# A 16-head sparse attention stage joined to the input product in front of it, and a block boundary placed after a down projection

## The chip, the cores and the metric

The kernel runs on one core of a Trainium2 chip. A core has five instruction streams that run side by side and meet only at semaphores: TensorE (PE, matrix products and transposes), VectorE (DVE), ScalarE (ACT), GpSimd (POOL) and SyncE (SP, which issues the DMAs). The metric is the device time of one execution in microseconds, lower is better.

## What is computed

Two transformer blocks over 512 tokens of width 1024. The change touches the second block: its first mixer `mixer_ab`, and the place behind its first feed-forward part. Cut to what matters:

```python
def mixer_ab(h, w_in, ...):
    xr, gr, q, kc, vc, ks, vs, kw, vw, gl = jnp.split(h @ w_in, splits, axis=-1)
    y_rnn = rg_lru(causal_dwconv(xr, conv_w, conv_b), w_r, b_r, w_i, b_i, lam) * jax.nn.gelu(gr)
    y_att = nsa(q, kc, vc, ks, vs, kw, vw, gl, ...)     # 16 query heads, 4 key heads
    return jnp.concatenate([y_rnn, y_att], axis=-1) @ w_out

def rg_lru(x, ...):                                     # the recurrence
    ...
    u = jnp.sqrt(-jnp.expm1(2.0 * log_a)) * (i * x)
    ...                                                 # h_t = a_t * h_(t-1) + u_t, a scan over the 512 tokens

# nsa, for each token: gated sum of three attentions
    o = g[..., 0:1] * o_c + g[..., 1:2] * o_s + g[..., 2:3] * o_w   # compressed, 4 chosen blocks, window of 256

for i in range(2):                                      # second_block
    x = x + (1.0 + g_m) * rms_norm(mixer(h), norm_mix_post[i])
    h = rms_norm(x, norm_ffn_pre[i]) * (1.0 + sc_f) + sh_f
    x = x + (1.0 + g_f) * rms_norm(conv_ffn(h), norm_ffn_post[i])
```

## The kernel before

Activations are feature-major: a tile is 128 features by 512 tokens. A product walks over its output tiles; each takes 8 or more weight tiles, each split into a high and a low part (L327, L329, on DVE, from the six-slot `ring` into the three-slot `high`), and three matmuls per weight tile (L375 to L377, `passes`).

The program is a row of *blocks*. A block holds a program for each engine, and at its end all engines wait for one another (a barrier). `together` makes one block out of several stages: every engine runs its part of stage 1, then of stage 2, and so on, and only semaphores order the engines. The order on an engine is the order in which the code is written; nothing reorders it. Between blocks `k.next_stages()` starts a new set of semaphores, and `clear_previous` has POOL set the old ones to zero.

Three blocks matter here. **Block A** holds `ffn_up(0)`, `down_0`, the normalization `double_edge`, and `ab_front`: the input product `ab_in` (37 output tiles) with the recurrence and the compressed attention woven between its tiles. In `ab_front`, `evacuate(j)` (ACT, L2580) copies output tile j out of PSUM. The recurrence has 8 tiles of channels. Its last steps for each tile i are: `root` (ACT, square root, L2641), `open_out` (ACT, GELU of the gate, L2645), `scan` (DVE, one multiplication L2827 and the scan L2828), `multiply` (POOL, L2907), `high_part` (ACT, rounding to the high half, L2649) and `low_part` (DVE, the low half by subtraction, L2832). For tiles 4 to 7 the scans, and for all tiles `high_part` and `low_part`, stand behind the last output tile of the product, each in a loop of its own.

**Block B** is `sparse_attention`. It has 64 *items*: 8 pairs of heads (p), 4 groups of 128 query tokens (i), and b = 0 (chosen blocks) or 1 (window). Item m = 8p + 2i + b. Its width is the number of 128-key pieces: i + 1 for b = 0, at most 3 for b = 1, so that the widths of a pair are 1, 1, 2, 2, 3, 3, 4, 3. What an item needs:

- `scores` (PE, L2969): two matmuls into PSUM;
- the two reductions (DVE, L3053): add the mask, find the row maximum, write `rows`;
- two exponentials (ACT, L3084) with row sums;
- `norm` (DVE): a reciprocal (L3029) and two scalings (L3034);
- `transposes` (PE, L2982), `keep` (ACT, L3072, a copy out of PSUM), `values` (PE, L3004; the first of a pair also L2997).

The step m of each engine's program is, in this order:

```
PE:  scores(m+2)   transposes(m)   values(m-1)
DVE: reductions(m) norm(m-1)
ACT: exponentials(m)  keep(m-1)
```

Once a pair, ACT also runs `move` (L3077) and DVE `divide` (L387, L388). POOL writes the masks of the chosen blocks (`sel_bias`, L2950 and L2956) for pairs 0 to 3 at the start and for pairs 4 to 7 later. The masks lie in `k.high`, the place of the weights' high parts, which is free then.

**Block C** holds everything behind: `ab_out`, `ffn_norm_1` (an `edge`), `up_1`, `down_1`, `sc_norm` (an `edge`), the short convolution, two more products, `up_2`, `down_2` and the output. An `edge` (L463) is the passage from one product to the next. PE sums squares (L485, L488), ACT takes the root (L508), DVE inverts it (L530), PE spreads it (L477), and so on; `keep_busy` (L668) fills PE's gaps. ACT writes the last squares and the last output tile of the product ahead (L2333, L2335 in `plain_product`).

## Time and profile before

| | us |
|---|---|
| median of 3 runs | 2582.23 (2580.28 to 2588.74) |
| the profiled execution: time, span | 2582.75, 2580.9 |
| block B with the barrier ahead of it, on PE | 1360.6 to 1514.0 |
| PE busy in the whole span | 2417.4 (94%) |
| DVE, ACT, POOL busy | 1754.6 (68%), 665.7 (26%), 196.4 (8%) |

The profile is one execution; times in it are counted from the start of its span. A row of a timeline gives start, duration, engine, line and operation; in brackets stands how long the engine was idle before and whose instruction ended that. A barrier shows as a wait for a branch (L191 is the end of a block made by `together`). Instructions are pipelined: one may start shortly before the record of the one ahead ends.

### The profile page before, as it was taken

What the parts mean: (1) busy time and instruction counts of PE and PEld (TensorE: products, weight loads), DVE (VectorE), ACT (ScalarE), POOL (GpSimd) and SP (SyncE); (2) the same over time, 40 slices, a digit from 0 to 9 for tenths busy, and PEclk for the clock granted to TensorE, in tenths of its full rate; (3) what the DMA queues carried; (4) which work ended last, traced back from release to release, by engine and by line L of the source; (5) the groups of instructions that cost most, each with busy time, mean ns of one, the idle gap of its engine ahead of it and who ended that gap; (6) DMA issues with size and microseconds to landing.
All of it is one profiled execution on the core that took longest, in us unless ns stands there. A gap on an engine that the chain in (4) does not pass through costs nothing. (4 is left out here: it accounts for less than half of the span.)

```text
span 2580.9 us, 34064 instructions
## 1 busy us (share of the span) xinstructions
PE 2417.4 (94%) x13808; PEld 1957.6 (76%) x13808; DVE 1754.6 (68%) x2720; ACT 665.7 (26%) x1234; POOL 196.4 (8%) x169
## 2 busy tenths in 40 slices
PE   8997767798999999999988989999999999999997
PEld 6885766596688888787765568888888888888886
DVE  7674663774788886557787867766666886666653
ACT  3212432102111120221466741322211212322200
POOL 0002430200100001000021001000010001000000
PEclk9998976899999999999998999999999999999999
DMA  5220001241223345422220036233375353233342
GB/s 187 74 66 1 3 2 50 82 139 58 66 90 98 98 136 192 137 91 74 62 69 1 2 109 225 66 98 98 93 245 176 113 192 128 74 98 98 119 139 68
DMA packets 70332, 252.80 MB, mean 98 GB/s; under 512 B 7808, under 2 KB 8096, under 8 KB 69664
## 3 DMA queue, kind: packets, MB, share of 16 engines
q1 hardware_dynamic: 69888, 250.08, 29.4%
q8 instruction: 110, 1.80, 0.3%
q10 hardware_dynamic: 288, 0.54, 0.1%
q14 instruction: 46, 0.38, 0.0%
HBM read 248.50 MB, written 2.10 MB: 97 GB/s over the span
## 5 line engine op out<-in xcount | busy, mean ns | idle before, releaser
L375 PE MATMUL psum<-rounded_n,rounded_high 128*128 128x512 f32 x1856 | 738.5, 398 | 5.1 <-DVE rounded_n_low L559 1.8
L376 PE MATMUL psum<-rounded_n_low,rounded_high 128*128 128x512 f32 x1856 | 725.8, 391 | 0.0
L377 PE MATMUL psum<-rounded_n,rounded_ring 128*128 128x512 f32 x1856 | 725.5, 391 | 0.0
L329 DVE TENSOR_TENSOR rounded_ring<-ring,rounded_high 128x1024 fp32r<-128x1024 f32 (+1 forms) x360 | 444.6, 1235 | 12.4
L375 PEld LDWEIGHTS psum<-rounded_n,rounded_high 128*128 128x128 f32 x1856 | 350.8, 189 | 86.5 <-issue 8.5
L376 PEld LDWEIGHTS psum<-rounded_n_low,rounded_high 128*128 128x128 f32 x1856 | 350.8, 189 | 77.5 <-issue 5.8
L377 PEld LDWEIGHTS psum<-rounded_n,rounded_ring 128*128 128x128 f32 x1856 | 350.5, 189 | 73.8
L327 DVE CAST rounded_high<-ring 128x1024 fp32r<-128x1024 f32 (+1 forms) x360 | 246.4, 684 | 220.2 <-PE psum L377 211.7
L375 PE MATMUL psum<-rounded_arena,rounded_high 128*128 128x512 f32 x720 | 281.3, 391 | 4.4 <-DVE rounded_ring L329 4.4
L376 PE MATMUL psum<-rounded_arena,rounded_high 128*128 128x512 f32 x720 | 281.0, 390 | 0.0
L377 PE MATMUL psum<-rounded_arena,rounded_ring 128*128 128x512 f32 x720 | 280.9, 390 | 0.0
L2259 DVE SCALAR_TENSOR_TENSOR scratch<-arena,vecs,scratch 128x512 f32<-128x512 f32 x88 | 65.8, 748 | 162.8 <-ACT scratch L2246 162.8
L375 PEld LDWEIGHTS psum<-rounded_arena,rounded_high 128*128 128x128 f32 x720 | 135.7, 189 | 33.3 <-DVE rounded_ring L329 4.7
L376 PEld LDWEIGHTS psum<-rounded_arena,rounded_high 128*128 128x128 f32 x720 | 135.7, 188 | 28.2
L377 PEld LDWEIGHTS psum<-rounded_arena,rounded_ring 128*128 128x128 f32 x720 | 135.7, 188 | 28.2
L2240 ACT COPY arena<-psum 128x512 f32<-128x512 f32 x88 | 51.6, 587 | 351.2 <-PE psum L377 351.2
L2246 ACT ACTIVATE scratch<-arena,vecs 128x512 f32<-128x512 f32 x88 | 63.8, 725 | 201.1 <-DVE arena L2280 199.6
L2333 ACT ACTIVATE scratch<-psum 128x512 f32<-128x512 f32 x32 | 19.2, 600 | 322.0 <-PE psum L377 322.0
L428 POOL COPY sum_sq<-scratch 128x512 f32<-128x512 f32 x6 | 4.8, 802 | 1059.8 <-ACT scratch L2333 831.5
L431 POOL TENSOR_TENSOR sum_sq<-sum_sq,scratch 128x512 f32<-128x512 f32 x38 | 58.2, 1531 | 300.8 <-ACT scratch L2333 242.7
L785 DVE CUSTOM_DVE_ANT_0 arena<-arena 128x1024 f32<-128x1024 f32 x48 | 62.0, 1333 | 14.4 <-DMA arena<-in_mod_w 14.4
L785 DVE CUSTOM_DVE_ANT_0 n_low<-n_low 128x1024 f32<-128x1024 f32 x48 | 56.7, 1221 | 19.7 <-DMA n_low<-in_mod_w 19.7
(472 smaller groups left out, 3035.0 us busy)
## 6 DMA issues: line engine op xcount, KB each, us to landing
ring<-in_w_up SPq DMA_DIRECT2D x132, 512.0 KB, 3.5
ring<-in_w_down SPq DMA_DIRECT2D x48, 512.0 KB, 3.5
n_low<-in_mod_w SPq DMA_DIRECT2D x48, 512.0 KB, 5.5
arena<-in_mod_w SPq DMA_DIRECT2D x48, 512.0 KB, 5.3
ring<-in_w_ab_in SPq DMA_DIRECT2D x37, 512.0 KB, 3.5
ring<-in_w_mix_in SPq DMA_DIRECT2D x31, 512.0 KB, 3.5
ring<-in_w_sc_in SPq DMA_DIRECT2D x24, 512.0 KB, 4.9
ring<-in_w_down SPq DMA_DIRECT2D x24, 384.0 KB, 3.2
```

The lines of the kernel that those rows point to most:

```text
L327: nc.vector.tensor_copy(self.rounded(high), raw).then_inc(self.weights_rounded, 1)
L329: nc.vector.tensor_tensor(self.rounded(raw), raw, self.rounded(high), ALU.subtract).then_inc(self.weights_split, 1)
L375: self.nc.tensor.matmul(out, w_high, x_high, start=first, stop=False)
L376: self.nc.tensor.matmul(out, w_high, x_low, start=False, stop=False)
L377: return self.nc.tensor.matmul(out, w_low, x_high, start=False, stop=last)
L428: nc.gpsimd.tensor_copy(total, sq).then_inc(added, 1)
L431: nc.gpsimd.tensor_tensor(total, total, sq, ALU.add).then_inc(added, 1)
L785: k.nc.vector.tensor_tensor_reduce(out=self.tiles[:, i % 3], in0=self.tiles[:, i % 3], in1=self.cond, scale=1.0, scalar=0.0, op0=ALU.mult, ...
L2240: nc.scalar.copy(x, k.psum[:, j % PRODUCT_BANKS, :]).then_inc(out, 1)
L2246: nc.scalar.activation(dst, x, ACT.Copy, scale=taps[:, col:col + 1]).then_inc(tapped, 1)
L2259: link(nc.vector.scalar_tensor_tensor(dst, src[:, 0:T], taps[:, col:col + 1], dst, ALU.mult, ALU.add))
L2333: nc.scalar.activation(k.squares[:, j % 2, :], k.psum[:, j % PRODUCT_BANKS, :], ACT.Square).then_inc(squared, 1)
```

## The change

Four things.

1. `sparse_attention` becomes a stage of block A. The barrier between them goes. PE starts the first scores when all 37 output tiles are evacuated (`out`), the queries and keys are rotated and the values are kept; POOL's masks wait until the gates are made and the last product tile is used. `k.rows` lies in `k.n_low` in place of `k.scratch`, which the recurrence still holds.
2. The recurrence's last steps move into the first 12 steps of the attention. In steps 0 to 3 DVE runs the scans of tiles 4 to 7 behind `norm(m-1)`. In steps 4 to 11 ACT runs `high_part(m-4)` behind `keep(m-1)`, and DVE runs `low_part(m-4)`, which waits for it, behind `norm(m-1)`. POOL runs `multiply` of tiles 4 to 7 after the masks of pairs 0 to 3. The GELUs of tiles 4 to 6 go ahead of `evacuate(36)`, that of tile 7 behind it.
3. Block C is cut in two behind `down_1`; `sc_norm` and what follows form a block of their own. `sc_in`'s modulation no longer waits for that of `down_1`.
4. The DVE stages of a block share one semaphore for their step-by-step waits (`vector_link`) in place of one each. The scans get a semaphore `scaled` of their own.

```diff
@@ ab_front
             if j == 36:
                 for i in range(4, 8):
                     root(i)
+                for i in range(4, 7):
+                    open_out(i)
             evacuate(j)
-        for i in range(4):
-            high_part(i)
-        for i in range(4, 8):
-            open_out(i)
-        for i in range(4, 8):
-            high_part(i)
+        open_out(7)
+
+    def finish_scalar(act, step):
+
+        if step >= 4:
+            i = step - 4
+            act.wait_ge(multiplied, i + 1)
+            nc.scalar.copy(k.rounded(k.z[:, XR + i, :]), lru_t[i]).then_inc(halved, 1)
+
+    def finish_vector(dve, step):
+
+        if step < 4:
+            i = step + 4
+            dve.wait_ge(rooted, i + 1)
+            dve.wait_ge(gated_in, i + 1)
+            dve.wait_ge(risen_a, i + 1)
+            x = k.z[:, XR + i, :]
+            nc.vector.tensor_tensor(x, x, lru_t[i], ALU.mult).then_inc(scaled, 1)
+            dve.wait_ge(scaled, i + 1)
+            nc.vector.tensor_tensor_scan(lru_t[i], lru_r[i], x, 0.0, ALU.mult, ALU.add).then_inc(scanned, 1)
+        else:
+            i = step - 4
+            dve.wait_ge(halved, i + 1)
+            nc.vector.tensor_tensor(k.rounded(k.z[:, GR + i, :]), lru_t[i], k.rounded(k.z[:, XR + i, :]),
+                                    ALU.subtract).then_inc(lowered, 1)
...
-        for i in range(4, 8):
-            scan(i)
-        for i in range(KT):
-            low_part(i)
...
-        for i in range(KT):
+        for i in range(4):
             multiply(i)
...
+    def finish_pool(pool):
+        for i in range(4, KT):
+            pool.wait_ge(scanned, i + 1)
+            pool.wait_ge(gelu_done, i + 1)
+            nc.gpsimd.tensor_tensor(lru_t[i], lru_t[i], k.z[:, GR + i, :], ALU.mult).then_inc(multiplied, 1)
@@ sparse_attention, pool
+        pool.wait_ge(signals["gated"], TT)
+        pool.wait_ge(k.weights_used, k.product_done("ab_in", PRODUCTS["ab_in"][0] - 1))
...
+            if a == 0:
+                signals["finish_pool"](pool)
@@ sparse_attention, tensor
+        pe.wait_ge(signals["rotated"], signals["turned_parts"])
+        pe.wait_ge(signals["out"], signals["n_out"])
+        pe.wait_ge(signals["v_kept"], 4)
+        pe.wait_ge(signals["kept"], 4)
         scores(0)
         scores(1)
@@ sparse_attention, vector
             if m >= 1:
                 norm(m - 1)
+            if m < 12:
+                signals["finish_vector"](dve, m)
@@ sparse_attention, scalar
             if m >= 1:
                 keep(m - 1)
+            if m < 12:
+                signals["finish_scalar"](act, m)
@@ build
-        k.rows = k.scratch
-        k.next_stages()
-        sparse_attention(k)
+        k.rows = k.n_low
+        together(k, Stage(pool=k.clear_previous), up, down, norm, front, sparse_attention(k, front))
         k.next_stages()
...
         down_1 = plain_product(k, "down_1", k.hidden, k.n, mod, up_1)
+        together(k, Stage(pool=k.clear_previous), mixed, norm_1, up_1, down_1)
+        k.next_stages()
         norm_2 = edge(k, "sc_norm", down_1, mod_part(k, 0, 5), mod_part(k, 1, 1), mod_part(k, 1, 0), "sc_in", k.n)
...
-        together(k, Stage(pool=k.clear_previous), mixed, norm_1, up_1, down_1, norm_2, short, short_out, norm_3, up_2, down_2, norm_4,
+        together(k, norm_2, short, short_out, norm_3, up_2, down_2, norm_4,
                  store_output(k, norm_4))
```

In the orders below the lines are those of the changed kernel where the kernel after is shown: L2723 and L2725 are the multiplication and the scan (the scan is printed as SCALAR_TENSOR_TENSOR), L2713 is `high_part`, L2729 `low_part`, L3083 a reduction ("ISA"), L3059 and L3064 the reciprocal and scalings of `norm`, L3103 `keep`, L3115 an exponential, L2589 `evacuate`, L2654 `open_out`.

DVE before, from the last multiplication and scan of the recurrence to the first reductions of the attention:

```order
L2827 TENSOR_TENSOR arena<-arena,rstd 128x512
L2828 SCALAR_TENSOR_TENSOR rstd<-scratch,arena 128x512
L2832 TENSOR_TENSOR rounded_arena<-arena,rounded_arena 128x512 x4
L2832 TENSOR_TENSOR rounded_arena<-scratch,rounded_arena 128x512 x2
L2832 TENSOR_TENSOR rounded_arena<-sum_sq,rounded_arena 128x512
L2832 TENSOR_TENSOR rounded_arena<-rstd,rounded_arena 128x512
L191 UNCONDITIONAL_BRANCH
L3020 UNCONDITIONAL_BRANCH
L3053 ISA scratch,rest<-psum,high 128x128
```

DVE after, the end of step 3 and the whole of step 4:

```order
L3059 RECIPROCAL rest<-rest 128x2
L3064 TENSOR_SCALAR n_low<-n_low,rest,arena 128x256 x2
L2723 TENSOR_TENSOR arena<-arena,rstd 128x512
L2725 SCALAR_TENSOR_TENSOR rstd<-scratch,arena 128x512
L3083 ISA n_low,rest<-psum,high 128x384
L3083 ISA rest 128x1
L3083 ISA n_low,rest<-psum,high 128x384
L3083 ISA rest 128x1
L3059 RECIPROCAL rest<-rest 128x2
L3064 TENSOR_SCALAR n_low<-n_low,rest,arena 128x256 x2
L2729 TENSOR_TENSOR rounded_arena<-arena,rounded_arena 128x512
```

Each scan now stands between the scalings of one item and the reductions of the next, and the first subtraction stands behind the scalings of item 3.

ACT before, from the evacuation of the last output tile to the end of block A:

```order
L2580 COPY arena<-psum 128x512
L2649 CAST rounded_arena<-arena 128x512 x4
L2645 ACT_TABLE_LOAD
L2645 ACTIVATE arena<-arena 128x512 x4
L2649 CAST rounded_arena<-scratch 128x512 x2
L2649 CAST rounded_arena<-sum_sq 128x512
L2649 CAST rounded_arena<-rstd 128x512
L191 UNCONDITIONAL_BRANCH
```

ACT after, from the last GELUs over the start of the attention to step 5:

```order
L2654 ACTIVATE arena<-arena 128x512 x3
L2589 COPY arena<-psum 128x512
L2654 ACTIVATE arena<-arena 128x512
L3115 ACT_TABLE_LOAD
...
L3115 ACTIVATE n_low,rest<-n_low,rest 128x384 x2
L3103 COPY n<-psum 128x2x256
L2713 CAST rounded_arena<-arena 128x512
L3115 ACTIVATE n_low,rest<-n_low,rest 128x384 x2
L3103 COPY n<-psum 128x2x384
L2713 CAST rounded_arena<-arena 128x512
```

Three GELUs stand ahead of the last evacuation now, and each rounding stands behind the copy of the item's transposes.

## Rows read from the trace of the kernel before

**Rows 1.** The page's part 1: busy time of PE over the span

```profile
PE 2417.4 (94%) x13808; PEld 1957.6 (76%) x13808; DVE 1754.6 (68%) x2720; ACT 665.7 (26%) x1234; POOL 196.4 (8%) x169
```

**Rows 2.** Timeline of PE at the boundary of blocks A and B

```profile
1360.63 1.23 PE L2969 MATMUL psum<-arena 64*128 64x128 f32 x8 [16.46 <-PEq L191]
```

**Rows 3.** Timeline of DVE at the same boundary

```profile
1359.40 0.69 DVE L2832 TENSOR_TENSOR rounded_arena<-rstd,rounded_arena 128x512 fp32r<-128x512 f32 x1
1361.57 0.29 DVE L3053 CUSTOM_DVE_ANT_0 scratch<-psum,high 128x128 f32<-128x128 f32 x1 [1.48 <-PE psum L2969]
```

**Rows 4.** Timeline of ACT at the same boundary

```profile
1336.08 2.19 ACT L2645 ACTIVATE arena<-arena 128x512 f32<-128x512 f32 x4
...
1342.53 0.71 ACT L2641 ACTIVATE rstd<-rstd,floor 128x512 f32<-128x512 f32 x1
1344.21 0.58 ACT L2580 COPY arena<-psum 128x512 f32<-128x512 f32 x1 [0.98 <-PE psum L377]
...
1346.88 1.28 ACT L2645 ACT_TABLE_LOAD   x1
...
1350.47 0.62 ACT L2649 CAST rounded_arena<-scratch 128x512 fp32r<-128x512 f32 x1
```

**Rows 5.** Busy time by stretch: stretch, length, busy us of each engine, granted clock (PEclk)

```profile
1350.00:1356.00 6.00, 0.00 (x0) 0.00 (x0) 5.93 (x4) 2.27 (x5) 5.91 (x4) 0.50 0.00 0
...
1369.00:1373.00 4.00, 4.00 (x16) 1.99 (x16) 1.85 (x7) 1.29 (x4) 0.00 (x0) 0.50 0.00 0
1373.00:1377.00 4.00, 4.00 (x34) 2.18 (x30) 3.09 (x10) 2.58 (x8) 0.00 (x0) 0.97 0.02 4
...
1400.00:1410.00 10.00, 10.00 (x86) 5.55 (x84) 7.04 (x32) 7.40 (x25) 0.00 (x0) 1.00 0.01 2
```

**Rows 6.** Timeline of DVE in pair 1, block B: items 8 to 13

```profile
1380.21 0.28 DVE L3053 CUSTOM_DVE_ANT_0 scratch<-psum,high 128x128 f32<-128x128 f32 x1
...
1385.78 0.60 DVE L3034 TENSOR_SCALAR scratch<-scratch,rest,arena 128x128 f32<-128x128 f32 x2
...
1389.28 0.56 DVE L3053 CUSTOM_DVE_ANT_0 scratch<-psum,high 128x384 f32<-128x384 f32 x1 [0.96 <-PE psum L2969]
...
1390.24 0.16 DVE L3029 RECIPROCAL rest<-rest 128x2 f32<-128x2 f32 x1
...
1392.36 0.87 DVE L3034 TENSOR_SCALAR scratch<-scratch,rest,arena 128x384 f32<-128x384 f32 x2
```

**Rows 7.** Timeline of PE in pair 1: transposes of widths 1 and 4

```profile
1384.77 0.44 PE L2982 MATMUL psum<-consts,scratch 128*128 128x128 f32 x2
...
1398.38 1.09 PE L2982 MATMUL psum<-consts,scratch 128*128 128x128 f32 x8
```

**Rows 8.** Timeline of ACT in pair 1: `keep` of widths 1 and 3

```profile
1385.24 0.37 ACT L3072 COPY n<-psum 128x256 f32<-128x256 f32 x1 [0.45 <-PE psum L2982]
...
1394.16 0.80 ACT L3072 COPY n<-psum 128x768 f32<-128x768 f32 x1 [0.35 <-PE psum L2982]
```

**Rows 9.** Timeline of DVE at the first scans, without and with POOL beside it

```profile
1304.68 0.68 DVE L2827 TENSOR_TENSOR arena<-arena 128x512 f32<-128x512 f32 x1
1305.40 1.22 DVE L2828 TENSOR_TENSOR_SCAN arena<-arena 128x512 f32<-128x512 f32 x1
1306.54 1.72 DVE L2827 TENSOR_TENSOR arena<-arena 128x512 f32<-128x512 f32 x1
1308.29 2.20 DVE L2828 TENSOR_TENSOR_SCAN arena<-arena 128x512 f32<-128x512 f32 x1
```

**Rows 10.** Timeline of POOL beside those scans

```profile
1305.94 1.76 POOL L2902 TENSOR_TENSOR arena<-arena,scratch 128x512 f32<-128x512 f32 x1 [5.29 <-ACT scratch L2624]
```

**Rows 11.** Busy time by stretch, as in rows 5, of an early stretch of small matmuls

```profile
392.00:400.00 8.00, 7.16 (x49) 5.26 (x50) 1.42 (x5) 0.99 (x1) 0.00 (x0) 0.50 0.00 0
```

**Rows 12.** Timeline of PE behind `down_1`

```profile
1988.30 1.05 PE L485 MATMUL psum<-consts,sum_sq 128*128 128x128 f32 x8
```

**Rows 13.** Timeline of ACT behind `down_1`

```profile
1988.99 0.58 ACT L2335 COPY n<-psum 128x512 f32<-128x512 f32 x1
```

More of the change, by code:

```diff
@@ L2001, in residual_product @@
     nc = k.nc
-    out, squared, added, steps, done = (k.sem(f"{name}_{s}") for s in ("out", "squared", "added", "steps",
+    out, squared, added, done = (k.sem(f"{name}_{s}") for s in ("out", "squared", "added",
                                                                        "done"))
@@ L2202, in ffn_up @@
     both = idx == 0
[L2203 to L2204 removed]
+    out, padded, tapped, gate_done, risen, hid_done = (
+        k.sem(f"{name}_{s}") for s in ("out", "padded", "tapped", "gate", "risen", "hid"))
     taps = k.vec(f"ffn_conv_{idx}")
@@ new lines, in pool @@
+    def pool(pool):
+        pool.wait_ge(signals["gated"], TT)
+        pool.wait_ge(k.weights_used, k.product_done("ab_in", PRODUCTS["ab_in"][0] - 1))
+        made = 0
+        for a in range(2):
+            for i in range(TT):
+                if a:
+                    pool.wait_ge(maxed, 2 * (items.index((3, i, 0)) + 1))
+                for s in range(2):
+                    w = (i + 1) * P
+                    dst = k.sel_bias[s][i]
+                    nc.gpsimd.tensor_copy(
+                        dst[:, 0:w].rearrange("p (j x) -> p j x", x=HD),
+                        k.block_bias[:, i, 2 * a + s, 0:2 * (i + 1)].unsqueeze(2)
+                        .broadcast_to([P, 2 * (i + 1), HD])).then_inc(biased, 1)
+                    made += 2
+                    pool.wait_ge(biased, made - 1)
+                    nc.gpsimd.tensor_tensor(dst[:, w - P:w], dst[:, w - P:w], k.const("causal"), ALU.add
+                                            ).then_inc(biased, 1)
+            if a == 0:
+                signals["finish_pool"](pool)
@@ new lines, in vector, with norm, divide @@
+    def vector(dve):
+        link = Link(dve, steps)
+        def norm(m):
+            p, i, b = items[m]
+            w = keys(i, b)[1] * P
+            dve.wait_ge(risen, 2 * m + 2)
+            sums = k.stats[:, 1, row(m, 0):row(m, 0) + 2]
+            link(nc.vector.reciprocal(sums, sums))
+            for s in range(2):
+                h = 4 * group(p, s) + p % 4
+                e = k.rows[:, row(m, s), 0:w]
+                gate = k.gate_tok[:, i, 3 * h + 1 + b:3 * h + 2 + b]
+                nc.vector.tensor_scalar(e, e, k.stats[:, 1, row(m, s):row(m, s) + 1], gate,
+                                        ALU.mult, ALU.mult).then_inc(normed, 1)
+        def divide(p):
+            dve.wait_ge(moved, p + 1)
+            link(split(k, link, k.z[:, NQT + p, :], k.ab_low[:, p, :]))
+        for m, (p, i, b) in enumerate(items):
+            w = keys(i, b)[1] * P
+            dve.wait_ge(scored, m + 1)
+            if m >= ROWS:
+                dve.wait_ge(turned, m - ROWS + 1)
+            for s in range(2):
+                if b == 0:
+                    dve.wait_ge(biased, 2 * (2 * (p // 4 * TT + i) + s + 1))
+                    bias = k.sel_bias[s][i]
+                else:
+                    bias = k.const("window")[:, 384 - w:384]
+                nc.vector.tensor_tensor_reduce(
+                    out=k.rows[:, row(m, s), 0:w], in0=k.psum[:, 2 * (m % 2) + s, 0:w], in1=bias,
+                    scale=-scale, scalar=3e38, op0=ALU.add, op1=ALU.min,
+                    accum_out=k.stats[:, 0, row(m, s):row(m, s) + 1]).then_inc(maxed, 1)
+            if m >= 1:
+                norm(m - 1)
+            if m < 12:
+                signals["finish_vector"](dve, m)
+            if m % 8 == 5 and p >= 1:
+                divide(p - 1)
+        norm(len(items) - 1)
+        divide(PAIRS - 1)
@@ new lines, in scalar, with keep, move @@
+    def scalar(act):
+        def keep(m):
+            p, i, b = items[m]
+            w = keys(i, b)[1] * P
+            act.wait_ge(turned, m + 1)
+            if m >= PTS:
+                act.wait_ge(mixed, m - PTS + 1)
+            nc.scalar.copy(k.pt[:, 2 * (m % PTS):2 * (m % PTS) + 2, 0:w], k.psum[:, 4:6, 0:w]
+                           ).then_inc(kept, 1)
+        def move(p):
+            act.wait_ge(mixed, 8 * (p + 1))
+            nc.scalar.copy(k.ab_low[:, p, :], k.psum[:, 6 + p % 2, :]).then_inc(moved, 1)
+        for m, (p, i, b) in enumerate(items):
+            w = keys(i, b)[1] * P
+            for s in range(2):
+                act.wait_ge(maxed, 2 * m + s + 1)
+                e = k.rows[:, row(m, s), 0:w]
+                nc.scalar.activation(e, e, ACT.Exp, scale=-1.0, bias=k.stats[:, 0, row(m, s):row(m, s) + 1],
+                                     accum_out=k.stats[:, 1, row(m, s):row(m, s) + 1]).then_inc(risen, 1)
+            if m >= 1:
+                keep(m - 1)
+            if m < 12:
+                signals["finish_scalar"](act, m)
+            if m % 8 == 3 and p >= 1:
+                move(p - 1)
+        keep(len(items) - 1)
+        move(PAIRS - 1)
```

244 lines of the change are left out of this document (81 added, 163 removed).

## The prediction, made before the changed kernel ran

> **What bounds the kernel now.** I read the page's busy times first. PE is busy for 94% of the span [rows 1], so a change gains where PE is idle, and costs where PE is made to wait. Then I looked at PE's timeline for its longest idle time: 16.46 us between the last matmul of `ab_in` and the first scores of the attention, ended by the end of a block [rows 2]. PE stopped at 1360.63 - 16.46 = 1344.17. In this time ACT and DVE run the recurrence's last steps; DVE's last subtraction ends at 1360.09, and 0.54 us later PE starts [rows 2, 3]. That is the price of a barrier behind the last engine. Third, the busy time by stretch in block B: at full clock PE is busy 10.00 of 10 us, DVE 7.04, ACT 7.40 [rows 5]. So the attention is bound by PE, with a quarter of DVE and ACT free. Moving the last steps there looks like free work. Whether it is depends on who waits for whom within a step, and that I work out below.
>
> **Part 1, the gap.** PE may start scores(0) when tile 36 is evacuated. Its evacuation ran at 1344.21 [rows 4]. Now it stands behind three GELUs: ACT's last square root ends at 1342.53 + 0.71 = 1343.24; a table load 1.28; three GELUs of 2.19 / 4 = 0.55 each, 1.64; the evacuation 0.58 [rows 4]. That is 1346.75. Scores of width 1 and the semaphores take some 0.65 (an estimate: two short matmuls of about the length of the transposes of width 1, 0.44 [rows 7], and two hand-overs), so the first reductions start at 1347.4 in place of 1361.57 [rows 3]: **14.2 us earlier**. POOL is no obstacle: before, the first mask was ready for DVE within 1361.57 - 1360.63 = 0.94 us of the block's start [rows 2, 3], and now the masks may start at 1344.2.
>
> **Part 2, steps 0 to 3: the scans.** DVE's own share of a step is two reductions and a `norm`. From pair 1: two reductions of width 1 take about 0.42, of width 3 0.96 (1389.28 to 1390.24); `norm` is 0.2 for the reciprocal and 0.60 (width 1) to 0.87 (width 3) for the scalings [rows 6]. For steps 0 to 3 that is 0.42, 0.42 + 0.80, 0.69 + 0.80, 0.69 + 0.93, in sum 4.8 us. Each step gets a multiplication and a scan: 1.86 from start to start (1304.68 to 1306.54 [rows 9]), four of them 7.4. DVE is then busy without a break: 12.1 us from the first reductions to those of item 4.
>
> **Part 3, steps 4 to 11: a new circle of waits.** Here the moved steps are small (rounding 0.62 on ACT [rows 4], subtraction 0.69 on DVE [rows 3]), but their places tie the engines together. In step m DVE's subtraction waits for ACT's rounding of the same step. On ACT that stands behind `keep(m-1)`, which waits for PE's `transposes(m-1)`, which wait for `norm(m-1)`, which DVE has just run. Behind the waiting subtraction on DVE are queued reductions(m+1) and norm(m), and so PE's next transposes. Before, DVE ran the reductions of the next item while PE transposed and ACT copied; now nothing overlaps. One turn at width 3: reciprocal, the first half of the scalings and the hand-over 0.2 + 0.44 + 0.1 [rows 6]; transposes 0.87 (0.44 at width 1, 1.09 at width 4 [rows 7]); `keep` 0.70 (record 0.80 [rows 8], of which the next instruction overlaps 0.1); rounding 0.60 with its hand-over; subtraction 0.75 with its hand-over; reductions of the next item 0.96; two further hand-overs 0.1. In sum 4.7 us. By widths, in the order of steps 4 to 11: 4.2, 5.0, 4.7, 4.7, 4.2, 3.4, 3.4, 4.2, together **33.9 us**. These are the times between one `norm` and the next, and as well those from the reductions of item 4 to those of item 12. Behind item 12 the order is the old one.
>
> So from the reductions of item 0 to those of item 12 the changed kernel needs 12.1 + 33.9 = 46.0 us. Before it was 27.7: 18.64 to item 8 (1361.57 to 1380.21), 9.07 on to item 12 (1389.28) [rows 3, 6]. **+18.3 us**. After that PE is the bound again and the rest is as long as before.
>
> **Part 4, POOL beside DVE.** POOL's masks and its four multiplications of tiles 4 to 7 now run beside DVE's scans. The scans show what that costs: 1.72 in place of 0.68 and 2.20 in place of 1.22 for the DVE instruction during which a POOL multiplication starts [rows 9, 10], 1.0 us each. Four multiplications: **+4.0 us** if each meets one DVE instruction (0 if they fall into DVE's waits in the circle, 6 if the masks collide too). The row shows a delay of 1.0 us for a POOL instruction of 1.76 us. The Trainium skill (SBUF — State Buffer, "SBUF: two separate sides") states an exclusive lock: whichever of the two engines begins holds the shared ports for its whole instruction, and the other is blocked. By that rule a POOL multiplication could cost DVE up to its full length, four of them 7.0 us, and the sum would be 3.0 us more.
>
> **Part 5, the clock.** After 16 us with PE idle the granted clock was 0.50, the lower level of 1.2 GHz; it came back at about 1373, after 12.8 us in which PE was busy nearly without a break [rows 2, 5]. Now PE is idle from 1344.2 to 1346.8, and does only some 1.5 us of work per 3 us step while DVE scans (an estimate: scores, transposes and values, each near the 0.44 of [rows 7]). I expect the clock to fall there too and to come back during the circle, when at half clock PE is nearly always busy. At half clock each transposing doubles, and it lies on the circle: with three turns at half clock (widths 2, 3, 3) 0.66 + 0.87 + 0.87 = **+2.4 us**. Bounds: 0, if it never falls; 5.9 for all eight turns, and about 5 more if PE's own work behind item 12 starts at half clock (the 12.8 us of [rows 2, 5] at half speed lose 6.4, less what DVE and ACT would not have followed).
>
> **Part 6, the new boundary.** Before, PE went from `down_1` straight to the sums at 1988.30 [rows 12]. Now it waits for ACT's last copy, 1988.99 + 0.58 = 1989.57 [rows 13], and the barrier of 0.54: 1990.1. **+1.8 us**. DVE's weight split of 1.9 us behind the barrier runs beside the sums, which take as long. The modulation's freed wait is worth nothing: SP's loads wait for the end of `down_1` anyway, and now for the barrier too. Bounds: 0.5 (a bare barrier) and 4, if the clock falls. The shared semaphore, the new `scaled` and the removed barrier's clearing add no instruction on PE: 0.
>
> **The sum.** -14.2 + 18.3 + 4.0 + 2.4 + 1.8 = +12.3 us. On the profiled execution's 2582.75 that is 2595.0; the median of the runs is 0.5 lower, so I predict **2594.5**. What a measurement of this kernel can tell from no change is about 0.3%, 7.7 us: slower means over 2590.
>
> **The rivals.**
> *The overlap works.* If DVE's subtraction found its rounded half ready, steps 4 to 11 would be bound by busy time: in 2 x 9.07 = 18.1 us DVE is free for some 30% [rows 5], 5.4 us, which takes up 8 x 0.72 = 5.8 us but for an estimated 1.6 us with imperfect packing, so that they last 19.7 us. The sum is -14.2 + (12.1 + 19.7 - 27.7) + 4.0 + 1.8 = -4.3: 2578. For it speaks DVE's 7.04 of 10 us [rows 5]; against it the order on ACT, in which the rounding stands behind the copy that itself waits for this step's `norm`. It decides from the point at which the halves are made a step earlier than they are used. 10%, with milder forms of it.
> *The circle at full clock and without collisions.* -14.2 + 18.3 + 1.8, and up to 2: 2588.5. 22%.
> *The clock stays at half through all twelve steps.* An early stretch of small matmuls had PE busy 7.16 of 8 us and stayed at 0.50 [rows 11]. Then part 5 is 5.9 + 5 = 10.9 in place of 2.4, the sum +20.8: 2603. Against it, the same mix of matmuls brought the clock back at 1373 [rows 5]. The Trainium skill (TensorE: Matmul & The Clock Gate, "Part 4: PE-mode transpose") says that transposes in that mode do not count as activity for the clock, which would favour this rival, as transposes are a third of the work. The stretch at 1400, with all three kinds mixed, ran at 1.00, which speaks against it as long as PE is dense. 20%.
> *The change does not do what it says*, that is, the first scores wait for something else to 1360. Nothing in the order does; under 2%, counted with the forecast.
>
> **How the numbers follow.** Forecast (2590 to 2599) 48%, half clock (to 2605) 20%, full clock (2584 to 2590) 22%, overlap (2575 to 2583) 10%. Leaving out the overlap and the top of half clock, the range is 2583 to 2605. Slower by over 0.3%: 0.48 + 0.20 and a little of the full-clock case, 0.70. Faster by over 0.3% (under 2574.5) needs the overlap and no collisions: 0.07. Within: 0.23.
>
> **What would show it.** In the profile after: first scores at about 1346.8 (part 1 wrong if later than 1350); first reductions of item 4 12 to 17 us behind those of item 0; between items 4 and 12 about 34 us or more, DVE idle ahead of each of eight subtractions for about 2 us with ACT's rounding as releaser, and ACT's `keep` waiting for PE in each step. If DVE does not wait there, part 3 is wrong and the kernel is faster. The granted clock in the stretch of the first twelve steps tells between the last two rivals; the lengths of the scans show part 4; the start of the sums behind `down_1` relative to ACT's last copy shows part 6.

## The result and the profile after

The changed kernel takes **2591.3 us** (median of 7 runs, 2589.02 to 2593.67), 1.0031 times the kernel before [1.0019, 1.0043], or 9.1 us more by the medians. It is slower, lies inside the range, and is 3.2 us under the forecast. The profiled execution took 2589.55 us with a span of 2587.6.

First the page's busy times, to be held against [rows 1]:

```profile
PE 2419.6 (94%) x13808; PEld 1958.2 (76%) x13808; DVE 1749.9 (68%) x2720; ACT 666.7 (26%) x1234; POOL 195.5 (8%) x169
```

All engines do the same work in the same shares. What changed is who waits for whom. PE's timeline at the old boundary, and the transposes of items 4 and 5:

```profile
1344.49 0.71 PE L2996 MATMUL psum<-arena 64*128 64x128 f32 x8 [2.61 <-issue]
...
1366.02 0.85 PE L3009 MATMUL psum<-consts,n_low 128*128 128x128 f32 x6 [1.91 <-DVE n_low L3064]
...
1370.90 1.51 PE L3009 MATMUL psum<-consts,n_low 128*128 128x128 f32 x6 [1.88 <-DVE n_low L3064]
```

The hole of 16.46 us [rows 2] has shrunk to 2.61 us. In its place PE is idle for 1.7 to 2.2 us ahead of the transposes of each of items 4 to 7, and for 0.3 to 2.3 us ahead of those of items 8 to 11; it waits there for DVE's scalings. DVE's timeline tells what DVE waits for: the first reductions, the first two subtractions (steps 4 and 5) with what lies between, and the first reductions of item 12:

```profile
1345.02 0.29 DVE L3083 CUSTOM_DVE_ANT_0 n_low<-psum,high 128x128 f32<-128x128 f32 x1 [5.22 <-PE psum L2996]
...
1363.63 0.69 DVE L2729 TENSOR_TENSOR rounded_arena<-arena,rounded_arena 128x512 fp32r<-128x512 f32 x1 [1.67 <-ACT rounded_arena L2713]
1364.24 0.55 DVE L3083 CUSTOM_DVE_ANT_0 n_low<-psum,arena 128x384 f32<-128x384 f32 x1
...
1365.20 0.16 DVE L3059 RECIPROCAL rest<-rest 128x2 f32<-128x2 f32 x1
1365.39 0.87 DVE L3064 TENSOR_SCALAR n_low<-n_low,rest,arena 128x384 f32<-128x384 f32 x2
1368.25 0.69 DVE L2729 TENSOR_TENSOR rounded_arena<-arena,rounded_arena 128x512 fp32r<-128x512 f32 x1 [1.99 <-ACT rounded_arena L2713]
1368.86 0.68 DVE L3083 CUSTOM_DVE_ANT_0 n_low<-psum,high 128x512 f32<-128x512 f32 x1
...
1394.48 0.55 DVE L3083 CUSTOM_DVE_ANT_0 n_low<-psum,high 128x384 f32<-128x384 f32 x1
```

And ACT's, for step 5: the copy `keep` waits for PE's transposes, and the rounding stands behind it.

```profile
1366.90 0.80 ACT L3103 COPY n<-psum 128x768 f32<-128x768 f32 x1 [0.76 <-PE psum L3009]
1367.60 0.62 ACT L2713 CAST rounded_arena<-arena 128x512 fp32r<-128x512 f32 x1
```

This is the circle of the prediction's part 3, row by row: scalings at 1365.39, transposes at 1366.02, copy at 1366.90, rounding at 1367.60, subtraction at 1368.25. DVE's eight waits for roundings are 1.67, 1.99, 2.65, 2.35, 2.36, 1.34, 1.34 and 1.67 us long, in sum 15.4.

The busy time by stretch, which answers to [rows 5] (last but two is the granted clock):

```profile
1350.00:1356.00 6.00, 3.75 (x12) 0.93 (x12) 5.93 (x10) 1.59 (x6) 4.58 (x5) 0.50 0.00 0
1361.00:1365.00 4.00, 2.39 (x18) 1.12 (x16) 2.30 (x9) 2.21 (x7) 0.49 (x1) 1.00 0.00 0
1369.00:1373.00 4.00, 2.12 (x14) 1.80 (x14) 2.11 (x7) 2.07 (x5) 0.00 (x0) 0.50 0.01 2
1381.00:1385.00 4.00, 3.84 (x26) 2.64 (x24) 1.60 (x9) 2.01 (x6) 0.00 (x0) 0.57 0.00 0
1400.00:1410.00 10.00, 9.30 (x95) 6.43 (x95) 7.88 (x35) 8.37 (x25) 0.00 (x0) 1.00 0.01 2
```

The clock fell at 1347, 2.5 us behind the first scores, rose at about 1361, fell again for the turn of step 6 (1367.4 to 1374.3) and part of that of step 8 (1381.1 to 1384.5), and stayed up from 1385.

Last the new boundary. ACT's last square and last copy of `down_1` (rows of ACT), and PE's sums (rows of PE), against [rows 12, 13]:

```profile
1993.57 0.60 ACT L2342 ACTIVATE scratch<-psum 128x512 f32<-128x512 f32 x1 [13.88 <-PE psum L386]
1994.06 0.58 ACT L2344 COPY n<-psum 128x512 f32<-128x512 f32 x1
```

```profile
1994.95 1.13 PE L494 MATMUL psum<-consts,sum_sq 128*128 128x128 f32 x8 [1.42 <-PEq L191]
```

The sums began 0.20 us ahead of the last square before (1988.50, ACT's row ahead of [rows 13]), and begin 1.38 us behind it now.

All stages beside their forecast, in us. "Reductions n" is the start of the reductions of item n. A turn is the time from one reciprocal of DVE to the next; the turn of step m has the scalings and transposes of item m - 1 in it. The expectations below say "turn of item 6" for that of step 6.

| stretch | before | after | change | forecast |
|---|---|---|---|---|
| last product matmul to reductions 0 | 17.39 | 3.14 | -14.25 | -14.2 |
| reductions 0 to reductions 4 | 9.10 | 15.04 | +5.94 | 12.1 + 4.0 for this stretch |
| reductions 4 to reductions 12 | 18.61 | 34.42 | +15.81 | 33.9 + 2.4 for this stretch |
| reductions 12 to the last `move` | 124.77 | 124.63 | -0.14 | 0 |
| last square of `down_1` to the sums | -0.20 | 1.38 | +1.58 | +1.8 |

The changes by the first three and the last stretch are -14.25 + 5.94 + 15.81 + 1.58 = +9.08, which is what the medians show. Nothing else moved: from the last `move` to the last square of `down_1` it is 474.45 us before and 474.46 after, and from the sums to the end 592.6 both times. The two profiled spans differ by only 6.7 us, since the product in this execution ended at 1341.88 and in that of before at 1344.17. Its end lay anywhere between 1337.5 and 1347.2 in the traces below, though none but experiments 3 and 9 moves anything near it, and none the blocks ahead. So the traces are compared from the product's end on.

### The profile page after: what moved, and what is told of

It is laid out like the page before. It is cut to its first block and busy times, and to the rows that moved or that the text cites. A ratio compares the mean times of both kernels' runs of the same rounds, so it can differ in the third digit from the quotient of the medians.

```text
span 2587.6 us, 34058 instructions
## 1 busy us (share of the span) xinstructions
PE 2419.6 (94%) x13808; PEld 1958.2 (76%) x13808; DVE 1749.9 (68%) x2720; ACT 666.7 (26%) x1234; POOL 195.5 (8%) x169
## 5 line engine op out<-in xcount | busy, mean ns | idle before, releaser
L384 PEld LDWEIGHTS psum<-rounded_arena,rounded_high 128*128 128x128 f32 x720 | 135.7, 188 | 33.4 <-DVE rounded_ring L338 4.7
L3009 PEld LDWEIGHTS psum<-consts,n_low 128*128 128x128 f32 x304 | 33.3, 144 | 55.6 <-issue 40.4
L3009 PE MATMUL psum<-consts,n_low 128*128 128x128 f32 x304 | 50.0, 293 | 24.7 <-DVE n_low L3064 24.3
```

Of the source, the lines that this page charges most:

```text
L384: self.nc.tensor.matmul(out, w_high, x_high, start=first, stop=False)
L3009: last = nc.tensor.transpose(k.psum[:, 4 + s, j * P:(j + 1) * P], k.rows[:, row(m, s), j * P:(j + 1) * P], k.const("ident"))
```

## The experiments

**Theory.** The merged block loses because DVE's subtraction and ACT's rounding of the same step stand in one circle with PE's transposes. **Rivals:** there is simply not enough free time on DVE (then no order helps), POOL's work beside DVE's, the clock, or the new boundary. The runs were made in three groups, and "before" is the kernel before, run again in each: 2581.8 us for experiments 1 to 4, 2583.4 for experiments 5, 6, 7 and 9, and 2582.8 for experiments 8 and 10. The changed kernel was 9.1 us above its own "before", so a version is held against it by its distance from the "before" of its group. The traces are compared by stretch, as above.

### 1. DVE subtracts one step later

```diff
-        else:
-            i = step - 4
+        elif step >= 5:
+            i = step - 5
             dve.wait_ge(halved, i + 1)
@@ sparse_attention, vector
-            if m < 12:
+            if m < 13:
```

> The changed kernel, but DVE subtracts one step later: in step m (5 to 12) it takes the half that ACT rounded in step m-1. All work is the same. Theory (a circle through norm, transposes, keep, rounding and subtraction): DVE no longer waits for the rounding, steps 4 to 11 shrink from 34.4 us to about 20 us, the total falls by 13 to 15 us to about 2577, below the kernel before. Rival 1 (the added instructions themselves fill DVE and ACT): the same work in the same steps, no change, 2591. Rival 2 (the low clock in the first steps is the cost): no change or up to 3 us less.

Measured: 2576.73 us, 0.9975 of before [0.9967, 0.9984]. That is 5.1 us under before where the changed kernel is 9.1 us over it, a gain of 14 us; from the product's end on, the trace gains 15.0. DVE's subtractions and a dense stretch:

```profile
1363.74 0.68 DVE L2729 TENSOR_TENSOR rounded_arena<-arena,rounded_arena 128x512 fp32r<-128x512 f32 x1
...
1366.54 0.68 DVE L2729 TENSOR_TENSOR rounded_arena<-arena,rounded_arena 128x512 fp32r<-128x512 f32 x1
...
1371.65 0.69 DVE L2729 TENSOR_TENSOR rounded_arena<-arena,rounded_arena 128x512 fp32r<-128x512 f32 x1 [0.35 <-ACT rounded_arena L2713]
```

```profile
1366.00:1370.00 4.00, 3.36 (x34) 2.44 (x32) 3.96 (x12) 4.00 (x11) 0.00 (x0) 1.00 0.00 0
```

The wait of 2 us ahead of each subtraction is gone (0.35 us is left in one step), and DVE and ACT are busy without a break in the stretch shown. Reductions 4 to 12 take 18.41 us in place of 34.42. The kernel before needed 18.61 without any of these steps, its first 2.6 us at the lower clock, and 18.33 for the next eight items at full clock. The last subtraction now stands behind the reductions of item 12, and from there to the last `move` it is 125.25 us (124.77 before). So eight roundings and eight subtractions fit into free time but for about half a microsecond; that free time was lacking falls as a rival. The loss in the circle was in the order alone.

### 2. ACT rounds ahead of the copy

```diff
@@ sparse_attention, scalar
-            if m >= 1:
-                keep(m - 1)
             if m < 12:
                 signals["finish_scalar"](act, m)
+            if m >= 1:
+                keep(m - 1)
```

> The changed kernel, but in each of steps 4 to 11 ACT rounds ahead of keep(m-1) instead of behind it. DVE still waits for the rounding of the same step, but the rounding no longer waits for PE's transposes. Theory of the circle: the turn is then reductions, two exponentials, rounding, subtraction: 3.2 us at width 3, 3.5 at width 4, 2.8 and 2.5 at widths 2 and 1, in sum about 24 us in place of 34.4; total 2581, between the changed kernel and the one with the later subtraction. Rival (the added work): 2591 as before. If only being late on ACT mattered and not the transposes, the gain would be that of one copy per step, about 0.6 us x 8 = 5 us: 2586.

Measured: 2580.95 us, 0.9995 of before [0.9986, 1.0004]; reductions 4 to 12 take 23.11 us, against 24 expected, 34.4 by the rival of the added work, and some 5 us less than 34.4 by that of the copy alone. DVE still waits, but for a shorter chain:

```profile
1361.10 0.69 DVE L2729 TENSOR_TENSOR rounded_arena<-arena,rounded_arena 128x512 fp32r<-128x512 f32 x1 [0.42 <-ACT rounded_arena L2713]
```

The rounding now waits only for ACT's exponentials. That cuts PE out of the circle and gives back 11.3 of 16 us; the lag of experiment 1 gives back the rest. Both edits leave all work in place.

### 3. The last steps back at the end of the product, one block kept

The subtractions, roundings, scans and multiplications stand where they stood before; `sparse_attention` stays in block A, and the new boundary stays.

```diff
+        for step in range(4, 8):
+            finish_scalar(act, step)
+        for i in range(4, 8):
+            open_out(i)
+        for step in range(8, 12):
+            finish_scalar(act, step)
@@ ab_front, vector
+        for step in range(12):
+            finish_vector(dve, step)
@@ ab_front, pool
+        finish_pool(pool)
```

> The changed kernel, but the recurrence's last steps stay ahead of the attention on DVE, ACT and POOL, as before the change; attention and input product are still in one block, and the boundary behind down_1 stays. Theory: the gap on PE was not the barrier but the 16 us of last steps; without the barrier DVE starts its first reductions about 1.4 us earlier, the new boundary costs 1.6 us: 2582.5, the same as the kernel before. Rival (the barrier with its drain and restart was worth several us): 2578 or less.

Measured: 2584.74 us, 1.0014 of before [1.0003, 1.0025], 2.9 us over before in place of the 0.7 or so that was expected. In the trace from the product's end on, -1.25 for the missing barrier, +0.55 up to reductions 12 and +1.58 for the new boundary make +0.9, inside the interval (0.8 to 6.5 us) at its lower end. So the barrier, with the scores that it held back, was worth only 1.25 us of the 17.4. PE's scores ran early, behind the product, and the scores of the next item waited for DVE:

```profile
1343.29 0.71 PE L3000 MATMUL psum<-arena 64*128 64x128 f32 x8 [0.72 <-issue]
...
1359.26 1.23 PE L3000 MATMUL psum<-arena 64*128 64x256 f32 x4 [15.26 <-DVE rest L3087]
```

The gap was DVE's and ACT's chain of last steps, and not the boundary.

### 4. The new boundary alone, in the kernel before

```diff
+        together(k, Stage(pool=k.clear_previous), mixed, norm_1, up_1, down_1)
+        k.next_stages()
         norm_2 = edge(k, "sc_norm", down_1, ...)
```

> The kernel before with only the third part of the change: the block boundary behind down_1. Theory: PE's sums start behind ACT's last copy and a barrier, 1.6 us later, and nothing else moves: 2583.8, 1.6 us above the kernel before. Rival (a boundary costs more further on, by the clock or by late weights and modulation loads): 4 us or more.

Measured: 2583.24 us, 1.0007 of before [0.9996, 1.0018]. The time cannot be told from no change. The trace can: PE's sums (first fence) against ACT's last square and copy (second).

```profile
1985.96 1.13 PE L485 MATMUL psum<-consts,sum_sq 128*128 128x128 f32 x8 [1.42 <-PEq L191]
```

```profile
1984.58 0.60 ACT L2333 ACTIVATE scratch<-psum 128x512 f32<-128x512 f32 x1 [13.88 <-PE psum L377]
1985.07 0.58 ACT L2335 COPY n<-psum 128x512 f32<-128x512 f32 x1
```

1.38 us behind the last square, as in the changed kernel: +1.58 each time. Behind the sums the rest takes 592.6 us, as before, so the rival of a cost further on falls. The changed kernel without this boundary was not run.

### 5. POOL's multiplications held back until the scans are over

```diff
             if a == 0:
+                pool.wait_ge(maxed, 10)
                 signals["finish_pool"](pool)
```

> The changed kernel, but POOL begins its four multiplications of the last steps only when the reductions of item 4 are done, so that none of them can meet a scan. The stretch from the reductions of item 0 to those of item 4 was 15.0 us, 2.9 more than the 12.1 of DVE's own work. Theory (the excess is POOL's work beside DVE's, multiplications and masks): 12.5 to 13.5 us, the masks still colliding, and in the following stretch at most 1 us is given back, since the multiplications now stand beside the circle; time about 2589.5. Rival (the excess is something else, such as PE at half clock or ACT): the stretch stays at 14.5 to 15.5 and the time at 2591.

Measured: 2593.95 us, 1.0040 of before [1.0026, 1.0053], against the expectation of a gain. By the times it can't be told from the changed kernel (1.0031 [1.0019, 1.0043]); by the trace, from the product's end to the last `move`, it is 2.2 us worse. The stretch of the scans came out as expected, 12.73 us in place of 15.04. But the multiplications now meet DVE in the circle. DVE's scalings and subtraction of step 4 (first fence) beside POOL's multiplications (second):

```profile
1361.09 2.66 DVE L3065 TENSOR_SCALAR n_low<-n_low,rest,arena 128x256 f32<-128x256 f32 x2
1365.42 1.24 DVE L2729 TENSOR_TENSOR rounded_arena<-arena,rounded_arena 128x512 fp32r<-128x512 f32 x1 [1.67 <-ACT rounded_arena L2713]
```

```profile
1361.06 2.54 POOL L2936 TENSOR_TENSOR scratch<-scratch,arena 128x512 f32<-128x512 f32 x2 [6.70 <-DVE rest L3084]
```

The scalings took 2.66 in place of 0.77 us and the subtraction 1.24 in place of 0.69: the turn of step 4 is 6.63 us in place of 4.20. All that was taken away came back. Later the clock fell in other steps than in the changed kernel and cost 0.7 us in the turns of steps 8 and 11 and about 1.3 behind item 12 (125.94 us from there to the last `move`, against 124.63). So 2.3 us of the excess of steps 0 to 3 are shown to be the cost of POOL's multiplications; that the cost depends on where they land is shown as well.

### 6. PE kept busy through the first four items

Matmuls on constants into a free PSUM bank, whose results nobody reads.

```diff
+        def warm(pe, n):
+            for _ in range(n):
+                nc.tensor.matmul(k.psum[:, 7, 0:P], k.const("ident"), k.const("ones"), start=True, stop=True)
+        warm(pe, 14)
         pe.wait_ge(signals["out"], signals["n_out"])
...
+            if m < 4:
+                warm(pe, 10)
             transposes(m)
```

> The changed kernel with idle-time matmuls on PE (14 ahead of the wait for the last evacuations, 10 ahead of the transposes of each of the first four items), whose results nobody reads. Theory (the clock's fall in the first turns costs 0.5 to 1 us, as the turns of items 6 and 8 are longer than at full clock): granted clock 1.00 from 1350 to 1385, the stretch from the reductions of item 4 to those of item 12 33.4 to 33.9 us in place of 34.4, time 2590. By the prediction's part 5 it would be 2.4 us less: 32.0 and 2588.5. Rival: the added matmuls delay the transposes, 34.5 or more.

Measured: 2592.69 us, 1.0036 of before [1.0023, 1.0050], which can't be told from the changed kernel. The clock stayed at 1.00 up to 1359.9, where that of the changed kernel had been down since 1347. The scans' stretch shrank from 15.04 to 14.51, but it also began later: the idle work ahead of the first scores took 3.29 us, longer than the 2.61 that PE had to wait, and reductions 0 began 3.60 us behind the product in place of 3.14. From the product's end to reductions 4 it is 18.11 us against 18.18. So the full clock gained nothing in steps 0 to 3, where DVE is busy without a break (POOL's work met other instructions of DVE than before, which this comparison includes). PE's timeline shows the first idle work with the scores behind it, and then the price further on, the idle work ahead of the transposes of items 2 and 3:

```profile
1344.30 3.29 PE L3039 MATMUL psum<-consts 128*128 128x128 f32 x28
1347.52 0.71 PE L2996 MATMUL psum<-arena 64*128 64x128 f32 x8
...
1359.64 4.13 PE L3039 MATMUL psum<-consts 128*128 128x128 f32 x20
1363.61 0.60 PE L3009 MATMUL psum<-consts,n_low 128*128 128x128 f32 x4
...
1365.35 2.50 PE L3039 MATMUL psum<-consts 128*128 128x128 f32 x20
```

The clock fell all the same at 1359.9, with PE busy without a break since 1357.2, and 4.13 and 2.50 us of idle work now stood ahead of transposes that were due. Reductions 4 to 12 took 37.5 us in place of 34.42, all of it in the turn of step 4 (7.52 us in place of 4.20); step 6 met the lower clock as before (5.28). The expectation of 33.4 to 33.9 for the circle was wrong, because the experiment put its own cost on the path; it does not show what the clock costs in the circle, and experiment 10 does.

### 7. The same idle work in the version of experiment 1

The edits of experiments 1 and 6 together.

> The kernel in which DVE subtracts one step later (2576.7), with the same idle-time matmuls. Theory (with the circle broken the copies and transposes at half clock are hidden behind DVE): no gain, the stretches 15.0 and 18.4 us as before, 2576.5 to 2577. Rival (PE at half clock still holds the first items up): 1 us less in the first stretch, 2575.5.

Measured: 2578.80 us, 0.9978 of before [0.9969, 0.9987], which can't be told from experiment 1. The first stretch was again 14.51, begun 0.45 later; reductions 4 to 12 took 21.54 in place of 18.41. From the product's end to the last `move` the trace is 3.1 us longer than that of experiment 1, against the expectation of no gain and no loss. The stretch between the last `move` and the last square of `down_1`, which no edit touches, is 473.5 to 474.8 us long in the traces and took back 0.8 of it; such differences, and those between executions, are a likely reason, not shown, why the times of experiments 6 to 10 show less than their traces.

### 8. The same, for the first two items only

Experiment 7 with one bound changed.

```diff
-            if m < 4:
+            if m < 2:
                 warm(pe, 10)
```

> The kernel in which DVE subtracts one step later (2576.7), with idle-time matmuls only ahead of the wait for the last evacuations (14) and ahead of the transposes of items 0 and 1 (10 each), where PE has nothing else to do. Theory (the 3 us that the fuller version lost were the added matmuls ahead of items 2 and 3, in which PE was late already): the stretch from the reductions of item 0 to those of item 4 14.5 us in place of 15.0, that from item 4 to item 12 18.4 as in the version without them, time 2576.2. Rival (the clock falls later, just when PE must catch up): the stretch from item 4 to item 12 20 us or more, 2577.5 or more.

Measured: 2577.48 us, 0.9976 of before [0.9966, 0.9986], again not to be told from experiment 1; 14.51 us in the first stretch, 20.71 from reductions 4 to 12. Here no idle work stands ahead of items 2 and 3, and yet 2.3 us are lost in the trace up to the last `move`. The stretches tell why, the first behind the idle work and the second in the circle's place:

```profile
1354.00:1356.00 2.00, 1.60 (x9) 0.53 (x9) 1.97 (x3) 0.37 (x1) 0.26 (x1) 1.00 0.00 0
...
1364.00:1366.00 2.00, 2.00 (x6) 0.50 (x5) 0.75 (x2) 0.96 (x4) 0.00 (x0) 0.50 0.01 4
```

The low clock was not removed, it was moved: from 1347 to 1360 (experiment 1), where DVE is the bound, to 1357 to 1367, where PE must catch up and DVE (busy 0.75 of 2 us) waits for it. The rival holds by the stretch (20.71, its bound was 20), not by the time.

### 9. The GELUs of tiles 4 and 5 earlier, on top of experiment 1

```diff
             if j == 35:
-                for i in range(4):
+                for i in range(6):
                     open_out(i)
...
-                for i in range(4, 7):
-                    open_out(i)
             evacuate(j)
+        open_out(6)
         open_out(7)
```

> The kernel in which DVE subtracts one step later (2576.7), and the GELUs of tiles 4 and 5 run ahead of the square roots, those of 6 and 7 behind the last evacuation. ACT then evacuates the last tile some 3 x 0.55 = 1.6 us (and a table load less ahead of it, 1.28) earlier, and the first scores start up to 2.5 us earlier. Theory (the gap in front of the first scores is paid in full by PE): first reductions 1 us or less behind the last product matmul in place of 3.1, the rest equal, 2574.7. Rival (the exponentials, which now stand behind two GELUs and two table loads, take the place of the gap): less than 1 us gained, 2576 or more.

Measured: 2576.12 us, 0.9973 of before [0.9961, 0.9984]; it cannot be told from experiment 1. Reductions 0 began 1.25 us behind the product in place of 3.14, as expected. Reductions 0 to 4 then took 16.64 in place of 15.04, since item 0 waits for exponentials behind two table loads (DVE idle 0.85 us for ACT) and POOL's multiplications met other instructions of DVE; and the clock stayed down to 1370, so that reductions 4 to 12 took 20.7 in place of 18.41. In the trace the gain of 1.9 us was given back twice: from the product's end to the last `move` it is 2.0 us longer than experiment 1. The time is the rival's (2576 or more); of its cause the trace shows 0.85 us, the rest is POOL's and the clock's.

### 10. PE kept busy within the circle of the changed kernel

```diff
+            if 4 <= m < 9:
+                warm(pe, 5)
             transposes(m)
```

> The changed kernel with five idle-time matmuls on PE (0.6 us together, whose results nobody reads) ahead of the transposes of items 4 to 8, where PE is idle for 0.7 to 2.2 us in each turn. Theory (in the changed kernel the lower clock costs 0.64 us in the turn of item 6, whose transposes take 1.51 in place of 0.85, and 0.25 in that of item 8): granted clock 1.00 in those turns, turn of item 6 4.6 in place of 5.28, turn of item 8 4.2 in place of 4.46, the circle 33.5 in place of 34.4, time 2590.4. Rival 1 (the time does not hang on the transposes' clock): turns of 5.3 and 4.5 at full clock, 2591.3. Rival 2 (five matmuls do not keep the clock up): the clock falls as before and the turns stay.

Measured: 2592.56 us, 1.0033 of before [1.0023, 1.0044], 2 us over what was expected and not to be told from the changed kernel. PE's transposes in the turn of step 6, and two stretches:

```profile
1376.16 0.85 PE L3009 MATMUL psum<-consts,n_low 128*128 128x128 f32 x6 [1.29 <-DVE n_low L3070]
```

```profile
1376.00:1378.00 2.00, 1.84 (x22) 1.52 (x22) 0.40 (x2) 1.32 (x4) 0.00 (x0) 1.00 0.00 0
...
1400.00:1402.00 2.00, 1.58 (x10) 1.28 (x12) 1.96 (x8) 1.07 (x4) 0.00 (x0) 0.52 0.00 0
```

The transposes took 0.85 in place of 1.51, the turn of step 6 4.61 in place of 5.28, that of step 8 4.08 in place of 4.46, and the circle 33.39 in place of 34.42: the theory held there to 0.1 us, and rivals 1 and 2 fall. But the clock fell at 1400 instead, when PE was due to be the bound again, and from reductions 12 to the last `move` it took 126.8 us in place of 124.6. In the trace the gain of 1.0 was paid back with 2.2.

## Why the prediction was right, and where its sizes were off

**Part 1, the gap: right.** Forecast -14.2, measured -14.25. The last evacuation, the scores and the hand-overs came as summed. POOL was no obstacle.

**Part 2, DVE's own work in steps 0 to 3: right.** 12.1 was forecast (its terms add up to 12.2). In experiment 5, with POOL's multiplications out of the way, the stretch is 12.73; four of DVE's rows there are lengthened beside the masks, by 0.86 in all, as in the changed kernel (0.84, below), so 11.9 are DVE's own.

**Part 3, the circle: right in mechanism and size.** Forecast 4.2, 5.0, 4.7, 4.7, 4.2, 3.4, 3.4, 4.2 (33.8 as rounded). Measured, from reciprocal to reciprocal: 4.20, 4.88, 5.28, 4.58, 4.46, 3.43, 3.44, 4.16. The two that stand out, 5.28 and 4.46, are those at the lower clock. Without the clock's share (below) the sum is 34.42 - 1.0 = 33.4 against 33.9, and experiment 10 measured 33.39. That the circle is a matter of order, and not of busy time, is shown by experiments 1 and 2. The rival "the overlap works" fell for the changed kernel, but named its own condition rightly, that the halves be made a step before they are used: experiment 1 is that rival, even better than its 19.7 us for these steps (18.41).

**Part 4, POOL beside DVE: right in kind, over-sized by a quarter.** Forecast +4.0, four times 1.0. The prediction's step that failed is "if each meets one DVE instruction". DVE's rows of the changed kernel, from step 2 to the reductions of item 4:

```profile
1351.97 1.55 DVE L3064 TENSOR_SCALAR n_low<-n_low,rest,arena 128x128 f32<-128x128 f32 x2
1353.44 1.77 DVE L2723 TENSOR_TENSOR arena<-arena,sum_sq 128x512 f32<-128x512 f32 x1
...
1358.21 0.68 DVE L2723 TENSOR_TENSOR arena<-arena,rstd 128x512 f32<-128x512 f32 x1
...
1360.06 0.53 DVE L3083 CUSTOM_DVE_ANT_0 n_low<-psum,high 128x384 f32<-128x384 f32 x1
```

and POOL's beside them:

```profile
1352.08 2.57 POOL L2936 TENSOR_TENSOR scratch<-scratch,arena 128x512 f32<-128x512 f32 x2
...
1356.54 1.27 POOL L2936 TENSOR_TENSOR sum_sq<-sum_sq,arena 128x512 f32<-128x512 f32 x1 [1.89 <-DVE sum_sq L2725]
1360.23 1.27 POOL L2936 TENSOR_TENSOR rstd<-rstd,arena 128x512 f32<-128x512 f32 x1 [2.41 <-DVE rstd L2725]
```

The first two multiplications cost DVE 0.95 (1.55 for 0.60) and 1.09 (1.77 for 0.68), the third 0.30 (a scaling of 1.04 for 0.74), the fourth nothing: it fell beside reductions, which stay at 0.53 and 0.55. In sum 2.34, and experiment 5 took 2.31 away. The masks, for which I had taken 0, cost 0.84 in four rows of 0.14 to 0.35. Together 3.2 by the rows, 2.9 by the stretch. The Trainium skill (SBUF — State Buffer, "SBUF: two separate sides") would have an exclusive lock for a whole instruction, 7.0 us for the four by my reading of it in the prediction; the measured 2.34 is a third of that. This doesn't decide whether the lock is exclusive: the first two multiplications cost DVE 2.04 of the 2.57 us that they took, and the last two ran in great part or wholly beside reductions. The same section limits the lock to DVE instructions in a two-port mode or with two inputs in SBUF, and the trace agrees with that: the reductions, with one input in PSUM, were not lengthened.

**Part 5, the clock: right that it falls and comes back, over-sized.** Forecast +2.4 for three turns at the lower clock. It was one whole turn (step 6, 0.66 us: transposes of 1.51 for 0.85) and part of one (step 8, 0.38 us: 4.46 for the 4.08 that the full clock gives in experiment 10), in sum 1.04; experiment 10 took away 1.03. The step that failed is the number of turns: the clock was back at 1361, ahead of the circle, and then fell twice within it, for 6.8 and 3.4 us, which the prediction did not foresee. The rival of twelve steps at half clock fell. The bound "about 5 more if PE's own work behind item 12 starts at half clock" was the right thing to fear, since experiments 5 and 10 show that case with 1.3 and 2.2 us.

**Part 6, the boundary: right.** Forecast +1.8, measured +1.58 here and in experiment 4. PE starts 0.31 us behind ACT's last copy (1994.64 to 1994.95), where I had taken 0.54.

So the forecast of +12.3 is +9.1 with 0.8 to 1.1 less for POOL, 1.4 less for the clock, 0.2 less for the boundary and 0.5 less for the turns. None of these cancels another. The measured time lies between the forecast and the rival "full clock and no collisions" (2588.5), as both of its disputed terms were there and smaller than forecast.

## What to carry to other kernels

When small steps are moved into another stage's loop, free time on the engines is not enough: follow one turn through all in-order engines, and if a step is made on one engine and used on another in the same turn, let the user lag by one turn (here 16 us for a changed index). A barrier's wait is mostly the chain behind it, so ask what the engines do during it before removing it: here the barrier was 1.25 of 17.4 us. And a gain ahead of a stage that PE will bound is only kept if the clock is up when that stage begins.

## What the runs showed of the hardware

- In experiment 6 PE was busy 1.14 of 2 us from 1356 to 1358, without a break from there, and the clock fell at 1359.9, in the middle of dense work. Keeping PE busy moved the low stretch, and in part shortened it, but did not remove it: 1347 to 1360 without idle work (experiment 1), 1357 to 1367 in experiment 8, 1358.1 to 1361.5 in experiment 7, and in experiment 10 from the turns of steps 6 and 8 to 1400. What sets the place is left open.
- The slowing of POOL and DVE is mutual. POOL's mask copies of 384 and 512 elements took 1.43 and 1.54 us beside a scan, and 0.50 and 0.61 without one. Of DVE's instructions, scalings, multiplications, subtractions and scans were lengthened by POOL, by up to 1.1 us for one multiplication of 1.27; reductions of a PSUM tile were not.
- The unchanged work ahead of the product's end moved by up to 9.7 us between profiled executions (1337.5 to 1347.2), more than most effects here. A single span does not show an effect of 2 us; the same stretch in two traces shows it far better (15.04 us for the scans' stretch in three traces of the same code).
